# A fourth pair by seven products in nine feed-forward groups, two more weight slots, and the residual kept in DRAM meanwhile

## The chip, the cores and the metric

The kernel runs on one core of a Trainium2 chip. The metric is the device time of one execution in microseconds, as the median of several runs. Before the change it is 1207.95 us (three runs, 1207.74 to 1208.55).

## What is computed

One decoder layer on 256 tokens of width 2048, all in float32. A mixer (mLSTM and retention heads with a common input and output projection) comes first and is not touched by the change. The part that is:

```python
h = rmsnorm(x, g_ffn_pre[l])
ff = (jax.nn.silu(h @ w_gate[l]) * (h @ w_up[l])) @ w_down[l]
x = x + rmsnorm(ff, g_ffn_post[l])
```

`D_FF` is 5632, so `w_gate` and `w_up` are 2048 x 5632 and `w_down` is 5632 x 2048. `x` in the last line is the residual: the input plus the normed mixer output.

## The kernel before

**Products in parts.** Every operand of a matmul is split into a high part (rounded to the matmul's number format by a copy) and a low part (the value less its high part). A product A x B is then three matmuls: high x high, high x low, low x high. Activations are split once. Weights are split as they stream in: SyncE (SP) loads them from DRAM into `raw` (four chunks), ScalarE writes the high part to a slot of `w_hi` (ACT.Copy), VectorE subtracts and writes the low part to the same slot of `w_lo`, the TensorE multiplies and counts `sub_done`. There are `AHEAD = 4` slots of 128 x 1024; ScalarE may fill a slot again when `sub_done` says that the sub-block that used it is finished. Each engine takes its instructions in the order of its program.

**Groups.** The 5632 columns of gate and up are done in 11 groups of 512 (`FF_GROUPS`). Group 0 stands apart, in two plain rounds. Groups 1 to 10 go over the 2048 rows in eight *pairs* of 128-row tiles. The two weight matrices, the two tiles of a pair and the two halves of the tokens make a 2 x 2 by 2 x 2 block product for each pair. `Plan` (L59) says for each pair how it is done:
- "R": eight products, in two sub-blocks (up, then gate) of 12 matmuls of 128x512 each; 24 matmuls.
- "S": seven products of sums of blocks (a Strassen-Winograd scheme), in four pieces with 2, 1, 2 and 2 products; 6, 3, 6 and 6 matmuls, 21 together. The sums on the token side are made once per S pair, before group 1 (`seven_sums`, `seven_lo`). The sums on the weight side are made for each group anew, in `raw` itself.

Groups 1 to 9 use `FULL`, group 10 uses `FINAL`. `w_down` follows in two halves of 22 pairs (`DOWN`, `LAST_HALF`), six of them S in each; there the token sums are made along the way.

**An S pair, step by step.** The pair's raw chunk holds four blocks of 512 columns: b12, b22, b11, b21.
- ScalarE, `unit_hi` (L955): the high part of piece 0 (b22, b11), of piece 1 (b21), of piece 2 (after L622 and L1558), of piece 3 (after L624 and L626). The copy is on L976, for an R pair on L965.
- VectorE, `unit_lo` (L1541): the low part of piece 0 (L1550), then the sum L1558 (b12 + b11 after L622, written over b11), then the low parts of pieces 1, 2 and 3 (L1550). For an R pair: two low parts on L1547.
- GpSimd, `weight_sums` (L617): L622 (b22 - b12, as soon as the up half of the chunk has arrived), L624 (b22 - b11, after L1558), L626 (b21 - b11, after the low part of piece 1).
- TensorE, `seven_piece` (L2019): waits for the low part of each piece.

**The order within a group** is written out by hand in `ff_group`, once per engine. On VectorE (L1574), around the low parts of group i with number m: `partial_sums` of group i-1 before m = 1 (L1561), `up_sums` before m = 2, `gate_sums` before m = 3 (it waits until the TensorE has finished group i-1), `gated` before m = 4 (in group 1 `first_gated`, which waits for the whole round before), `turned_lo` after m = 5 (it follows eight transposes on the TensorE, L1986, and `turned_hi` on ScalarE). Before m = 4 there are always six R sub-blocks from pair 7 of the group before on.

**Loads.** SP issues them in order (`unit_rows`, L544): pair n + 4 is loaded into the chunk of pair n once VectorE has written the last low part of pair n. Up and gate halves are 512 KB each.

**The residual.** `resid` (L230, 16 KB per partition) holds x, from L1410 on x plus the mixer's result. The TensorE transposes it and ScalarE squares it while group 0 runs; nothing reads it after that until the last four adds for each token half (L1702), whose results SP stores to `out`.

Of the kernel before, what the change touches and what calls it, by code (L numbers as in the profile page):

```python
# [30 lines left out]
P = 128  # L31
SEQ = 256
# [23 lines left out]
SEVEN = (2, 4, 6)  # L56
# [13 lines left out]
FULL = Plan("RRSRSRSR")  # L70
FINAL = Plan("RRSRSRRR")
# [144 lines left out]
def hybrid_layer(nc, x, positions, g_mix_pre, w_in, conv_w, conv_b, b_igate, b_fgate, g_mlstm_head,  # L216
                 g_ret_head, w_out, g_mix_post, g_ffn_pre, w_gate, w_up, w_down, g_ffn_post,
                 inv_freq, out):
    with ExitStack() as ctx:
# [10 lines left out]
        resid = sb("resid", [P, TT, D])  # L230
# [77 lines left out]
        def s_upper(j):  # L308

            return s_hi[:, j] if j < 2 else s_third[:, 0]  # L310

        def s_lower(j):

            if j == 2:
                return s_third[:, 1, 0:2, :], s_third[:, 1, 2:4, :]
            return s_lo12(j), s_lo34[:, j]
# [88 lines left out]
        resid_ready = sem("resid_ready")  # L405
        h_ready = sem("h_ready")
# [72 lines left out]
        def _(sp):  # L479
# [163 lines left out]
        def _(act):  # L643
# [311 lines left out]
            def unit_hi(i, odd, plan, m):  # L955

                n, piece = plan.pieces[m]
                q, slot, arrived = chunk_of(i, n), ff_slot(i, odd, m), up_arrived(i, n)
                act.wait_ge(sub_done, ff_base(i) + (m - 3))
                if plan.units[n] == "R":  # L960
# [4 lines left out]
                    act.activation(w_hi[:, slot, :], raw[:, q, SUB * piece:SUB * (piece + 1)],  # L965
# [10 lines left out]
                act.activation(slot_blocks(w_hi, slot, piece), seven_blocks(piece, q),  # L976
# [1149 lines left out]
```

## Time and profile before

| | us |
|---|---|
| median of the runs | 1207.95 |
| the profiled execution | 1214.75 |
| its span, first to last instruction | 1213.0 |
| granted clock of the TensorE, mean | 0.997 |

The profile is of one execution. Times in it count from the first instruction. Engines: PE is the TensorE's matmul, PEld its weight load, DVE is VectorE, ACT is ScalarE, POOL is GpSimd, SPq is SyncE's queue of DMA issues. In a row of the timeline the first number is the start, the second the time taken (of several instructions, if it ends in x2 or x3), and the bracket at the end is the idle time of the engine before it, with what ended it. The rows in question stand below, in groups.

### The profile page before, as it was taken

How to read it: one execution, taken by the hardware profiler on the slowest of the kernel's cores; microseconds unless marked ns; L12 is line 12 of the kernel's file. 1: busy time of each engine (PE TensorE's matmuls, PEld its weight loads, DVE VectorE, ACT ScalarE, POOL GpSimd, SP SyncE). 2: the span in 40 equal slices, each digit the busy share in tenths (PEclk: the TensorE clock that was granted, in tenths of full speed). 3: DMA queues.
4: the chain of work that ended last, by engine and by line, in shares of the span. 5: the costliest groups of instructions: out<-in, count | busy, mean ns of one | idle time of the engine just before them, and what ended most of it. 6: DMA issues, size and time to landing. Idle time of an engine off the chain costs nothing.

```text
span 1213.0 us, 16357 instructions
## 1 busy us (share of the span) xinstructions
PE 1193.4 (98%) x5760; PEld 998.9 (82%) x5760; DVE 937.1 (77%) x1230; ACT 678.0 (56%) x896; POOL 214.3 (18%) x158
## 2 busy tenths in 40 slices
PE   8999999999899999999999999999999999999997
PEld 7888888888788888888888888888888878888885
DVE  6657777877677745868887888888788788879887
ACT  5654666474564744665556555555555555546553
POOL 1000100000000000004234333323433023313320
PEclk9999999999999999999999999999999999999999
DMA  8656867767676655545565566556556665564552
GB/s 314 210 148 159 213 180 150 180 142 198 163 163 184 216 200 187 180 158 203 187 208 169 202 207 207 193 187 211 172 206 208 212 215 206 197 210 158 206 199 98
DMA packets 122723, 230.67 MB, mean 190 GB/s; under 512 B 8104, under 2 KB 24752, under 8 KB 122032
## 3 DMA queue, kind: packets, MB, share of 16 engines
q1 hardware_dynamic: 122208, 226.85, 60.4%
q0 software_dynamic: 464, 3.15, 0.6%
q8 instruction: 30, 0.49, 0.2%
q14 instruction: 21, 0.17, 0.0%
HBM read 227.88 MB, written 2.11 MB: 190 GB/s over the span
## 4 chain that ended last, share of the span: by engine, by line
PE 89%; DMA 5%; DVE 3%; ACT 1%; issue 1%; POOL 0%; SPq 0%; DVEq 0%; ACTq 0%
PE bank L1709 88%; DMA raw<-in_w_in 4%; DVE w_lo L1067 1%; PE bank L1986 1%; DMA resid<-in_x 1%; ACT w_hi L656 1%; PE bank L1714 0%; PE bank L1903 0%; DVE h L1094 0%; DVE w_lo L1550 0%; DVE gT L1281 0%; DVE resid L1702 0%; ACT w_hi L976 0%; PE bank L1959 0%; DVE pre L1254 0%
## 5 line engine op out<-in xcount | busy, mean ns | idle before, releaser
L1709 PE MATMUL bank<-w_hi,h2T 128*128 128x512 f32 x1126 | 359.3, 390 | 0.0
L1067 DVE TENSOR_TENSOR w_lo<-raw,w_hi 128x1024 fp32r<-128x1024 f32 x172 | 209.7, 1224 | 131.4 <-ACT w_hi L656 130.6
L656 ACT ACTIVATE w_hi<-raw 128x1024 fp32r<-128x1024 f32 x172 | 180.6, 1058 | 181.6 <-PE bank L1709 154.8
L1550 DVE TENSOR_TENSOR w_lo<-raw,w_hi 128x1024 fp32r<-128x1024 f32 (+1 forms) x164 | 216.2, 1323 | 73.6 <-ACT w_hi L976 72.5
L1709 PE MATMUL bank<-hT,w_hi 128*128 128x512 f32 x768 | 271.3, 397 | 1.2 <-DVE w_lo L1067 1.2
L976 ACT ACTIVATE w_hi<-raw 128x1024 fp32r<-128x1024 f32 (+1 forms) x164 | 156.4, 954 | 168.0 <-PE bank L1709 139.9
L1709 PEld LDWEIGHTS bank<-w_hi,h2T 128*128 128x128 f32 x1126 | 211.4, 188 | 43.9
L1709 PE MATMUL bank<-hT,w_lo 128*128 128x256 f32 x768 | 214.6, 279 | 0.0
L1709 PE MATMUL bank<-w_lo,h2T 128*128 128x512 f32 x543 | 211.3, 389 | 0.0
L1547 DVE TENSOR_TENSOR w_lo<-raw,w_hi 128x1024 fp32r<-128x1024 f32 x166 | 198.0, 1224 | 15.8 <-ACT w_hi L965 14.3
L965 ACT ACTIVATE w_hi<-raw 128x1024 fp32r<-128x1024 f32 x166 | 169.9, 1055 | 67.3 <-PE bank L1709 65.0
L1709 PE MATMUL bank<-w_hi,ffT 128*128 128x512 f32 x584 | 184.3, 389 | 0.0
L1709 PEld LDWEIGHTS bank<-hT,w_hi 128*128 128x128 f32 x768 | 144.1, 188 | 33.6 <-DVE w_lo L1067 1.5
L1709 PEld LDWEIGHTS bank<-hT,w_lo 128*128 128x128 f32 x768 | 145.0, 189 | 0.0
L1709 PEld LDWEIGHTS bank<-w_hi,ffT 128*128 128x128 f32 x584 | 109.6, 188 | 23.0 <-DVE w_lo L1547 0.3
L624 POOL TENSOR_TENSOR raw<-raw 128x512 f32<-128x512 f32 x41 | 65.2, 1591 | 339.2 <-DVE raw L1558 339.2
L1709 PEld LDWEIGHTS bank<-w_lo,h2T 128*128 128x128 f32 x543 | 102.0, 188 | 21.0
L1709 PE MATMUL bank<-w_lo,ffT 128*128 128x512 f32 x292 | 113.6, 389 | 0.0
L622 POOL TENSOR_TENSOR raw<-raw 128x512 f32<-128x512 f32 x41 | 71.6, 1747 | 204.0 <-DMA raw<-in_w_up 189.5
L1709 PE MATMUL bank<-w_hi,hT 128*128 128x512 f32 x256 | 81.3, 393 | 0.9 <-DVE w_lo L1067 0.9
L1709 PE MATMUL bank<-w_hi,mixT 128*128 128x512 f32 x256 | 80.2, 391 | 0.0
L626 POOL TENSOR_TENSOR raw<-raw 128x512 f32<-128x512 f32 x41 | 66.5, 1623 | 6.3 <-DVE w_lo L1550 6.3
(232 smaller groups left out, 1264.4 us busy)
## 6 DMA issues: line engine op xcount, KB each, us to landing
raw<-in_w_in SPq DMA_DIRECT2D x63, 1024.0 KB, 10.6
raw<-in_w_down SPq DMA_DIRECT2D x88, 512.0 KB, 5.0
raw<-in_w_up SPq DMA_DIRECT2D x80, 512.0 KB, 4.0
raw<-in_w_gate SPq DMA_DIRECT2D x80, 512.0 KB, 4.8
raw<-in_w_out SPq DMA_DIRECT2D x16, 1024.0 KB, 5.1
raw<-in_w_gate SPq DMA_DIRECT2D x4, 1024.0 KB, 5.2
raw<-in_w_up SPq DMA_DIRECT2D x4, 1024.0 KB, 5.9
resid<-in_x SPq DMA_DIRECT2D x2, 1024.0 KB, 7.2
```

Source lines behind the costliest of these rows:

```text
L622: pool.tensor_tensor(b12, b22, b12, ALU.subtract).then_inc(t3_ready, 1)
L624: pool.tensor_tensor(b22, b22, b11, ALU.subtract).then_inc(t14_ready, 1)
L626: pool.tensor_tensor(b21, b21, b11, ALU.subtract).then_inc(t14_ready, 1)
L656: act.activation(part_of(w_hi, rnd, s), src, ACT.Copy).then_inc(hi_done, 1)
L965: act.activation(w_hi[:, slot, :], raw[:, q, SUB * piece:SUB * (piece + 1)], ACT.Copy).then_inc(hi_done, 1)
L976: act.activation(slot_blocks(w_hi, slot, piece), seven_blocks(piece, q), ACT.Copy).then_inc(hi_done, 1)
L1067: dve.tensor_tensor(part_of(w_lo, rnd, s), raw_sub(rnd, s)[1], part_of(w_hi, rnd, s).bitcast(F32), ALU.subtract).then_inc(lo_done, 1)
L1547: dve.tensor_tensor(w_lo[:, slot, :], raw[:, q, SUB * piece:SUB * (piece + 1)], w_hi[:, slot, :].bitcast(F32), ALU.subtract).then_inc(lo_d ...
L1550: dve.tensor_tensor(slot_blocks(w_lo, slot, piece), seven_blocks(piece, q), slot_blocks(w_hi, slot, piece).bitcast(F32), ALU.subtract)\
L1709: return pe.matmul(out_, lhsT, rhs, start=start, stop=stop, skip_group_check=True)
L1986: ins = pe.transpose(bank[:, b0 + j // 2, c:c + P], ff(t)[:, j * P:(j + 1) * P], ident)
```

## The change

- `SEVEN`, the S pairs of groups 1 to 9, goes from (2, 4, 6) to (2, 3, 5, 6), and `FULL` from RRSRSRSR to RRSSRSSR; a group has 24 sub-blocks and pieces in place of 22. `FINAL` (group 10) keeps two S pairs, now pairs 2 and 3.
- The slots of `w_hi` and `w_lo` go from four to six in the feed-forward part. The two new ones, `more_hi` and `more_lo`, lie over `resid`.
- SP copies `resid` to a DRAM scratch (two transfers of 1 MB) behind the loads of the first round and before those of group 1, and back when eight sub-blocks are left. ScalarE waits for the first (`spilled`) before it fills slot 4 the first time, VectorE for the second (`resid_back`) before the last adds. The last eight sub-blocks use four slots again.
- The token sums are made for four S pairs; the fourth's high and low parts (`s_fourth`) take the place of spare space.

The diff, cut to its core (what is left out passes the new slot lists to where `w_hi` and `w_lo` stood, drops an argument of `ff_slot`, and puts `len(SEVEN)` where 3 stood):

```diff
-SEVEN = (2, 4, 6)
+SEVEN = (2, 3, 5, 6)
+FF_SLOTS = 6
+END_SUBS = 8
...
-FULL = Plan("RRSRSRSR")
-FINAL = Plan("RRSRSRRR")
+FULL = Plan("RRSSRSSR")
+FINAL = Plan("RRSSRRRR")
...
+def at_end(i, m):
+
+    return isinstance(i, int) and i == FF_GROUPS + 1 and m >= DOWN.subs - END_SUBS
+
+
-def ff_slot(i, odd, m):
-
+def ff_slot(i, m):
+
+    if at_end(i, m):
+        return m % AHEAD
     if down_half(i) is not None:
-        return (ff_base(i) + m) % AHEAD
-    return (m + (0 if odd else FULL.subs)) % AHEAD
+        return (ff_base(i) + m - FF_FIRST) % FF_SLOTS
+    return m % FF_SLOTS
+
+
+def slot_depth(i, m, first=False):
+
+    return AHEAD if at_end(i, m) or (first and m < AHEAD) else FF_SLOTS
...
-        resid = sb("resid", [P, TT, D])
+        resid_home = ExitStack()
+        resid = sb("resid", [P, TT, D], stack=resid_home)
+        resid_home.close()
+        more_hi = sb("more_hi", [P, FF_SLOTS - AHEAD, SUB], F32R)
+        more_lo = sb("more_lo", [P, FF_SLOTS - AHEAD, SUB], F32R)
+        resid_rows = nc.dram_tensor("resid_rows", (SEQ, D), F32)
...
+            sp.wait_ge(resid_ready, TT * CHUNKS)
+            for t in range(TT):
+                sp.dma_start(resid_rows.ap()[t * P:(t + 1) * P, :], resid[:, t, :]).then_inc(spilled, 16)
             for n in range(4):
                 unit_rows(1, n, FF_FIRST - 8 + FREE[n])
...
+            sp.wait_ge(sub_done, N_SUBS - END_SUBS)
+            sp.wait_ge(spilled, 16 * TT)
+            for t in range(TT):
+                sp.dma_start(resid[:, t, :], resid_rows.ap()[t * P:(t + 1) * P, :]).then_inc(resid_back, 16)
...
-            def unit_hi(i, odd, plan, m):
+            def unit_hi(i, odd, plan, m, first=False):
 
                 n, piece = plan.pieces[m]
-                q, slot, arrived = chunk_of(i, n), ff_slot(i, odd, m), up_arrived(i, n)
-                act.wait_ge(sub_done, ff_base(i) + (m - 3))
+                q, slot, arrived = chunk_of(i, n), ff_slot(i, m), up_arrived(i, n)
+                if first and m >= AHEAD and m < FF_SLOTS:
+                    act.wait_ge(spilled, 16 * TT)
+                act.wait_ge(sub_done, ff_base(i) + (m + 1 - slot_depth(i, m, first)))
...
-                    if first and 1 <= m < 4:
+                    if first and 1 <= m <= len(SEVEN):
                         seven_lo(m - 1)
...
                 lo(R_FF + 1, s + AHEAD)
-                if s:
-                    seven_sums(s - 1)
+                seven_sums(s)
...
+                if t == 0:
+                    dve.wait_ge(resid_back, 16 * TT)
```

## Rows read from the trace of the kernel before

**Rows 1.** The page of the kernel before, busy time by engine.
```profile
PE 1193.4 (98%) x5760; PEld 998.9 (82%) x5760; DVE 937.1 (77%) x1230; ACT 678.0 (56%) x896; POOL 214.3 (18%) x158
```

**Rows 2.** The chain of waits, 560 to 980 us: start, us, what.
```profile
594.78 0.87 PE bank L1986 x8
595.66 41.74 PE bank L1709 x183
...
936.73 42.21 PE bank L1709 x186
```

**Rows 3.** Waits, whole span: us in total, times, longest us.
```profile
PEld bank L1709 <- DVE w_lo L1550: 5.0, 13, 1.0
```

**Rows 4.** Timeline of VectorE, 664 to 708: start, us, what, idle before.
```profile
664.70 3.49 DVE L1547 TENSOR_TENSOR w_lo<-raw,w_hi 128x1024 fp32r<-128x1024 f32 x3
...
677.87 1.22 DVE L1550 TENSOR_TENSOR w_lo<-raw,w_hi 128x1024 fp32r<-128x1024 f32 x1
...
686.30 2.35 DVE L1547 TENSOR_TENSOR w_lo<-raw,w_hi 128x1024 fp32r<-128x1024 f32 x2
688.58 1.21 DVE L1550 TENSOR_TENSOR w_lo<-raw,w_hi 128x1024 fp32r<-128x1024 f32 x1
...
696.84 2.35 DVE L1547 TENSOR_TENSOR w_lo<-raw,w_hi 128x1024 fp32r<-128x1024 f32 x2
699.11 1.21 DVE L1550 TENSOR_TENSOR w_lo<-raw,w_hi 128x1024 fp32r<-128x1024 f32 x1
700.35 0.69 DVE L1558 TENSOR_TENSOR raw<-raw 128x512 f32<-128x512 f32 x1
700.96 0.68 DVE L1550 TENSOR_TENSOR w_lo<-raw,w_hi 128x512 fp32r<-128x512 f32 x1
702.59 1.29 DVE L1550 TENSOR_TENSOR w_lo<-raw,w_hi 128x1024 fp32r<-128x1024 f32 x1 [0.95 <-ACT w_hi L976]
706.16 1.23 DVE L1550 TENSOR_TENSOR w_lo<-raw,w_hi 128x1024 fp32r<-128x1024 f32 x1 [2.28 <-ACT w_hi L976]
707.31 1.22 DVE L1547 TENSOR_TENSOR w_lo<-raw,w_hi 128x1024 fp32r<-128x1024 f32 x1
```

**Rows 5.** Timeline of GpSimd, 664 to 708: start, us, what, idle before.
```profile
701.12 1.68 POOL L624 TENSOR_TENSOR raw<-raw 128x512 f32<-128x512 f32 x1 [5.30 <-DVE raw L1558]
702.75 2.29 POOL L626 TENSOR_TENSOR raw<-raw 128x512 f32<-128x512 f32 x1
```

**Rows 6.** Line L626, 560 to 965: ns min/median/max.
```profile
L626 POOL TENSOR_TENSOR raw<-raw x28: 1277/1294/2297, 564.3 to 947.9; 128x512 f32<-128x512 f32 x28
```

**Rows 7.** Timeline of ScalarE, 698 to 708.
```profile
701.50 1.06 ACT L976 ACTIVATE w_hi<-raw 128x1024 fp32r<-128x1024 f32 x1 [2.10 <-PE bank L1709]
705.07 1.06 ACT L976 ACTIVATE w_hi<-raw 128x1024 fp32r<-128x1024 f32 x1 [2.51 <-POOL raw L626]
```

**Rows 8.** Groups by line, 560 to 1213: busy us, mean ns, idle before.
```profile
L976 ACT ACTIVATE w_hi<-raw 128x1024 fp32r<-128x1024 f32 x120 | 127.3, 1061 | 138.9 <-PE bank L1709 110.9 <-POOL raw L626 26.6
```

**Rows 9.** Loads from `in_w_up`, 500 to 540: ns, first and last start.
```profile
L485 SPq DMA_DIRECT2D raw<-in_w_up x2: 368/368/368, 507.8 to 512.2; - x2
```

**Rows 10.** The page, DMA issues: KB each, us to landing.
```profile
resid<-in_x SPq DMA_DIRECT2D x2, 1024.0 KB, 7.2
```

**Rows 11.** Timeline of ScalarE, 530 to 550.
```profile
546.86 1.06 ACT L976 ACTIVATE w_hi<-raw 128x1024 fp32r<-128x1024 f32 x1 [1.66 <-PE bank L1709]
```

**Rows 12.** Timeline of VectorE, 1165 to 1213.
```profile
1201.94 1.42 DVE L1702 SCALAR_TENSOR_TENSOR resid<-ff_out,stat,resid 128x512 f32<-128x512 f32 x2
```

**Rows 13.** Busy time by engine in one group: stretch, us, engines, PEclk, DMA, GB/s.
```profile
719.70:762.30 42.60, 42.60 (x193) 35.07 (x192) 35.90 (x38) 24.17 (x28) 14.55 (x9) 1.00 0.58 197
```

**Rows 14.** The same view around 312 us.
```profile
280.00:322.00 42.00, 38.75 (x219) 33.87 (x218) 27.36 (x36) 18.18 (x27) 0.00 (x0) 0.96 0.66 183
312.20:313.00 0.80, 0.78 (x3) 0.79 (x4) 0.80 (x1) 0.00 (x0) 0.00 (x0) 0.50 0.00 0
```

**Rows 15.** Timeline of the TensorE, 311.5 to 313.
```profile
312.22 1.01 PE L1709 MATMUL bank<-v_sb,probs 128*128 x3 [3.25 <-DVE probs L1309]
```

More of the change, by code:

```diff
@@ L308, in s_upper @@
         def s_upper(j):
-            return s_hi[:, j] if j < 2 else s_third[:, 0]
+            return s_hi[:, j] if j < 2 else (s_third, s_fourth)[j - 2][:, 0]
         def s_lower(j):
-            if j == 2:
-                return s_third[:, 1, 0:2, :], s_third[:, 1, 2:4, :]
+            if j >= 2:
+                lower = (s_third, s_fourth)[j - 2]
+                return lower[:, 1, 0:2, :], lower[:, 1, 2:4, :]
             return s_lo12(j), s_lo34[:, j]
@@ L321, in seven_blocks @@
             return (blocks[:, 1:3, :], blocks[:, 3:4, :], blocks[:, 0::2, :], blocks[:, 1::2, :])[piece]
+        hi_slots = [w_hi[:, s, :] for s in range(AHEAD)] + [more_hi[:, s, :] for s in range(FF_SLOTS - AHEAD)]
+        lo_slots = [w_lo[:, s, :] for s in range(AHEAD)] + [more_lo[:, s, :] for s in range(FF_SLOTS - AHEAD)]
+        early_hi_slots = [early[:, 0, s, :] for s in range(AHEAD)]
+        early_lo_slots = [early[:, 1, s, :] for s in range(AHEAD)]
         def slot_blocks(w, slot, piece):
-            return w[:, slot, :].rearrange("p (a c) -> p a c", c=512)[:, 0:1 if piece == 1 else 2, :]
+            return w[slot].rearrange("p (a c) -> p a c", c=512)[:, 0:1 if piece == 1 else 2, :]
         def s_lo12(j):
@@ L964, in unit_hi @@
                         act.wait_ge(raw_full[q], arrived + 16 * (R_FF + 2))
-                    act.activation(w_hi[:, slot, :], raw[:, q, SUB * piece:SUB * (piece + 1)],
+                    act.activation(hi_slots[slot], raw[:, q, SUB * piece:SUB * (piece + 1)],
                                    ACT.Copy).then_inc(hi_done, 1)
@@ L975, in unit_hi @@
                     act.wait_ge(t14_ready, 2 * sums_index(i, n) + 2)
-                act.activation(slot_blocks(w_hi, slot, piece), seven_blocks(piece, q),
+                act.activation(slot_blocks(hi_slots, slot, piece), seven_blocks(piece, q),
                                ACT.Copy).then_inc(hi_done, 1)
@@ L989, in ff_group @@
                         first_product(i - 1, FULL, c0)
-                    unit_hi(i, odd, plan, m)
+                    unit_hi(i, odd, plan, m, first)
                     if m == 0 and first:
-                        act.wait_ge(s_summed, 3)
-                        for j in range(3):
+                        act.wait_ge(s_summed, len(SEVEN))
+                        for j in range(len(SEVEN)):
                             act.activation(s_upper(j), s_sum[:, j], ACT.Copy).then_inc(s_rounded, 1)
@@ L1753, in wide_columns, with sub_tokens @@
                         after(s)
-            def sub_tokens(count, slot, act_T, pair, k0, last, tiles=range(TT), w_hi=w_hi, w_lo=w_lo):
+            def sub_tokens(count, slot, act_T, pair, k0, last, tiles=range(TT), w_hi=hi_slots, w_lo=lo_slots):
                 pe.wait_ge(lo_done, count)
@@ L1762, in sub_tokens @@
                         lo_x = act_T[:, k, SEQ + t * P:SEQ + (t + 1) * P]
-                        mm(bank[:, 2 * pair + t, :], hi_x, w_hi[:, slot, w], k == 0, False)
-                        mm(bank[:, 2 * pair + t, :], hi_x, w_lo[:, slot, w], False, False)
-                        ins = mm(bank[:, 2 * pair + t, :], lo_x, w_hi[:, slot, w], False, k == last)
+                        mm(bank[:, 2 * pair + t, :], hi_x, w_hi[slot][:, w], k == 0, False)
+                        mm(bank[:, 2 * pair + t, :], hi_x, w_lo[slot][:, w], False, False)
+                        ins = mm(bank[:, 2 * pair + t, :], lo_x, w_hi[slot][:, w], False, k == last)
                 if TT - 1 in tiles:
@@ L2014, in products @@
                 w = slice(512 * c, 512 * (c + 1))
-                mm(bank[:, b, :], act_hi, w_hi[:, slot, w], first, False)
-                mm(bank[:, b, :], act_hi, w_lo[:, slot, w], False, False)
-                return mm(bank[:, b, :], act_lo, w_hi[:, slot, w], False, False)
+                mm(bank[:, b, :], act_hi, hi_slots[slot][:, w], first, False)
+                mm(bank[:, b, :], act_hi, lo_slots[slot][:, w], False, False)
+                return mm(bank[:, b, :], act_lo, hi_slots[slot][:, w], False, False)
             def seven_piece(i, odd, plan, m, c0, s0):
                 n, piece = plan.pieces[m]
-                k, slot = 2 * n, ff_slot(i, odd, m)
+                k, slot = 2 * n, ff_slot(i, m)
                 half = down_half(i)
```

34 lines of the change are left out of this document (18 added, 16 removed).

## The prediction

> **What bounds the kernel now.** I read the totals first [rows 1]: the TensorE is busy for nearly the whole span, VectorE for three quarters. That points at the TensorE, and the chain of waits seems to agree: through the feed-forward part it is one unbroken run of matmuls [rows 2]. A group of eight pairs with three done by seven products takes 183 matmuls in 41.74 us (0.228 us each) and 0.87 us for eight transposes, 42.6 us together; group 10, with two such pairs, has 186 matmuls in 42.21 us, only 0.227 us each. So a little waiting hides in the longer pitch, and the list of waits says for what: the weight loads waited for VectorE's low part of a seven-product piece 13 times, 5.0 us in all [rows 3]. A TensorE that runs straight into its supplier, group after group, calls for a look at the supplier's own period.
>
> That is in VectorE's timeline of one group [rows 4]. I call a pair done by seven products an S unit, the other an R unit. From 664.70 to 707.31, one period of 42.61 us, VectorE does this, in its order:
> - 664.70 to 677.87, 13.17 us: six low parts of R units (L1547) and the sums of the group before (L1561 to L1508);
> - S unit to 686.30, 8.43 us (with `turned_lo`); R unit to 688.58, 2.28; S unit to 696.84, 8.26; R unit to 699.11, 2.27; S unit to 707.31, 8.20.
>
> There is no idle time outside the S units. The period of this in-order chain equals the TensorE's: the two engines bound the group together.
>
> What an S unit's 8.2 us consist of is seen in the third one [rows 4 to 7]. Low part of piece 0 at 699.11; sum L1558 (700.35 to 701.04); low part of piece 1 at 700.96. GpSimd's L624 starts at 701.12 and ends at 702.80, and its L626 at 702.75 takes 2.29 us, though the shortest takes 1.28 [rows 5, 6]. Low part of piece 2 runs 702.59 to 703.88; only then does L626 get on (703.88 + 1.2 = 705.04). ScalarE's high part of piece 3 starts at 705.07 [rows 7], VectorE's low part at 706.16. So VectorE and GpSimd take turns, each finishing its instruction before the other goes on, and piece 3 comes through GpSimd and ScalarE one after another. VectorE's five instructions last 5.1 us of the 8.2 [rows 4]; for the rest it stands still, in order behind piece 3.
>
> **The change, part by part.** Matmuls: an R unit has 24, an S unit 21. One more S unit in nine groups removes 27 matmuls x 0.228 = 6.2 us of TensorE work. Group 10 keeps two S units, only in other places.
>
> VectorE's chain: S for R adds 8.26 - 2.27 = 5.99 us a group. The new order RRSSRSSR gives 13.17 + 8.43 + 8.26 + 2.28 + 8.26 + 8.20 = 48.60 us [rows 4], against a TensorE need of 180 x 0.228 + 0.87 = 41.9. The chain wins: nine groups x 5.99 = +53.9 us, and none of the 6.2 us is seen, since the TensorE is then the one that waits. I take 8.26, the unit followed by another subtraction L622; the bounds of one S unit are worked out under the rivals (7.2) and by the slowest seen (8.43).
>
> Group 10: the TensorE enters it behind VectorE's last low part by six matmuls of a piece 3 and one R unit, less VectorE's own R unit: 30 x 0.228 - 2.28 = 4.6 us. VectorE needs (13.17 - 2.28) + 8.43 + 8.26 = 27.6 us to the end of the second, now adjacent, S unit, after which the TensorE has 6 + 4 x 24 = 102 matmuls, 23.2 us: 50.8 - 4.6 = 46.2 us instead of 42.21 + 0.87 = 43.1. That is +3.1 us.
>
> Two more slots (six for four): they let ScalarE's high parts start earlier. The view of waits has large figures for this: L976 waited 110.9 us for the TensorE to free a slot [rows 8]. In the third S unit the high part of piece 2 did so until 701.50 [rows 7]. But freed of it, it could start at 701.04, when L1558 is done, and be over at 702.1, while L624 holds VectorE off until 702.80 anyway. The slot wait is a shadow of another one. Slots lengthen the lead, they don't shorten the chain: worth at most one time two R sub-blocks, 2 x 12 x 0.228 = 5.5 us, in group 1. There VectorE waits for the whole round before (`first_gated`), so I take 0.
>
> Residual out: the spill stands on SP behind the loads of the first round, whose last issue is at 512.2 [rows 9]. A transfer of 1 MB took 7.2 us [rows 10]; that last load and both halves of the residual one after another end by 512.6 + 3 x 7.2 = 534 us. ScalarE needs the new slots first for its fifth high part of group 1, at 546.86 [rows 11]. Hidden, with 12 us to spare. Queued behind the spill on SP are the loads of group 1's first units; if they have no slack they come one or two transfers late, once: 0 taken, 14 at most. Residual back: queued once the last eight sub-blocks are left, 96 x 0.227 = 21.8 us before the TensorE ends, so about 1183; landed by 1198, needed at 1201.94 [rows 12]. Hidden too, with 4 us to spare. The wait in front of it on SP has only the output stores behind it. The fourth unit's token sums and their rounding come once, before and in group 1: seven VectorE operations, none wider than L1558 with its 0.69 us [rows 4], so under 4.8 us, in a stretch where VectorE waits for the TensorE in `first_gated`: 0 taken.
>
> **Sum.** 53.9 + 3.1 = +57 us. The profiled execution took 1214.75 us (span 1213.0); the median of the runs is 6.8 lower, and I carry the difference over: 1207.95 + 57 = 1265 us.
>
> Put strictly, as turns that never overlap, VectorE's operations on two SBUF tensors and GpSimd's must fit into a group one after another: 20 low parts x 1.14 us (686.30 to 688.58 is two), 8 operations of half the width x 0.61 (700.35 to 700.96), 12 on GpSimd x 1.28 [rows 4, 6] are 22.8 + 4.9 + 15.4 = 43.1 us, more than the TensorE's 41.9. The Trainium skill, "SBUF — State Buffer", section "Who interferes with whom", has this as a rule: with two SBUF inputs VectorE takes a read interface that GpSimd also needs, and the one that comes second is blocked. By that rule alone a group would be at least 43.1 us, a time between before and my forecast; the trace agrees with the turns and adds the dependences that make it 48.6.
>
> **The rivals.**
> A. *The forecast*, VectorE's chain at 8.26 us an S unit. For it: period equals period, waits of the TensorE only for that piece. With each of the 36 S units 0.4 us shorter or 0.3 longer it gives 1250 to 1276.
> B. *The TensorE stays the bound; faster.* VectorE's busy time in a group is 35.9 us [rows 13]; with an S unit's work in place of an R unit's about 39 of 41.9, so there is room if its idle time goes with the slots. The time would be 1207.95 - 6.2 = 1202, or 1197 if the 5.0 us of waits go as well. It decides where the four S units take no more than (41.9 - 13.17 - 2.28)/4 = 6.6 us each. Against it: slots don't touch L624, L626 and piece 3, which make the 8.2; and the turns alone need 43.1 of 41.9 us.
> C. *A shorter S unit.* If with a high part ready earlier L626 follows L624 at once, it ends at 702.80 + 1.28 = 704.1, low part of piece 2 at 705.2 beside the high part of piece 3, low part of piece 3 at 706.3: 7.2 us. The group is then 13.17 + 2.28 + 33.15 - 4 x 1.0 = 44.6, +2.0 for nine groups and about 1 in group 10: 1227. Against it: with the low part of piece 2 already waiting, VectorE went first.
> D. *The clock falls.* New gaps of the TensorE, up to about 2 us before a piece 3, 6.7 us a group. In the trace the granted clock fell to 0.50 (1.2 GHz) about 312 us, after a wait of 3.25 us [rows 14, 15]; a mean of 0.96 over 42 us makes that 3.4 us at the lower level. 1.7 us lost after each adjacent pair, 18 times: +31 on top of A, 1296. Against: my gaps are shorter, and the TensorE has slack to take it up. The Trainium skill, "TensorE: Matmul & The Clock Gate", section "A second HAM failure mode: psum-queue depth-cycling", reports a kernel whose short, repeated idling made the clock swing.
>
> **How the numbers follow.** A 0.68, B 0.08, C 0.15, D 0.07, and 0.02 for a result within 0.2% of before (about what a measurement of this kernel can tell from no change). The forecast is A's. The range leaves out B and most of D: 1220, a little under C, to 1286. Faster by over 0.2% 0.08, within it 0.02, slower 0.90.
>
> **What would show it.** Right: groups 2 to 9 about 48.6 us apart, VectorE's order without idle time outside S units, 8.2 to 8.4 us each; the TensorE waiting for VectorE's low part (seven-product form) some 60 us in all; fewer waits of ScalarE for slots with nothing gained. Wrong: groups 42 us apart with S units near 6.6 (B), 44 to 45 (C), clock records at 0.5 in the groups (D), a wait on the spill ahead of group 1's fifth high part, or of the last adds for the residual.

## The result, and the profile after

The kernel after takes 1268.77 us (median of 4 runs, 1268.35 to 1269.14) against 1207.85 for the kernel before: a ratio of 1.0503, interval 1.049 to 1.0516, +60.9 us. Its profiled execution took 1268.9 us with a span of 1267.1.

| | before | after | forecast |
|---|---|---|---|
| time, us | 1207.85 | 1268.77 | 1265 |
| one group of 2 to 9, us | 42.64 | 48.65 in five of eight, 49.4 in three | 48.60 |
| S unit on VectorE, us | 8.2 to 8.4 | 8.2 to 8.5 | 8.2 to 8.4 |

The code of the feed-forward part has moved by some 35 lines: `unit_lo` is L1583 (R) and L1586 (S), its sum L1594, `turned_lo` L1552, `gated` L1544, GpSimd's three sums L656, L658, L660, ScalarE's high parts L1001 (R) and L1012 (S), the matmul L1746.

The page of the kernel after, busy time by engine, answers to [rows 1]:

```profile
PE 1209.0 (95%) x5733; PEld 1001.9 (79%) x5733; DVE 970.8 (77%) x1264; ACT 679.1 (54%) x915; POOL 268.4 (21%) x185
```

There are 27 matmuls fewer and yet more busy time on the TensorE; VectorE has the same share as before. From this view alone nobody would call VectorE the bound. Its timeline over one group does it (start, time taken, what, idle time before), and answers to [rows 4]:

```profile
677.00 2.35 DVE L1583 TENSOR_TENSOR more_lo<-raw,more_hi 128x1024 fp32r<-128x1024 f32 x2
...
690.16 1.22 DVE L1586 TENSOR_TENSOR more_lo<-raw,more_hi 128x1024 fp32r<-128x1024 f32 x1
...
694.27 1.29 DVE L1552 TENSOR_TENSOR ffT<-bank,ffT 128x512 f32 x2 [1.45 <-ACT ffT L972]
695.48 4.36 DVE L1586 TENSOR_TENSOR w_lo<-raw,w_hi 128x1024 fp32r<-128x1024 f32 x3
...
706.92 2.35 DVE L1583 TENSOR_TENSOR w_lo<-raw,w_hi 128x1024 fp32r<-128x1024 f32 x2
709.19 1.22 DVE L1586 TENSOR_TENSOR w_lo<-raw,w_hi 128x1024 fp32r<-128x1024 f32 x1
710.53 0.69 DVE L1594 TENSOR_TENSOR raw<-raw 128x512 f32<-128x512 f32 x1
711.14 0.69 DVE L1586 TENSOR_TENSOR w_lo<-raw,w_hi 128x512 fp32r<-128x512 f32 x1
712.41 1.65 DVE L1586 TENSOR_TENSOR more_lo<-raw,more_hi 128x1024 fp32r<-128x1024 f32 x1 [0.59 <-ACT more_hi L1012]
716.33 1.23 DVE L1586 TENSOR_TENSOR more_lo<-raw,more_hi 128x1024 fp32r<-128x1024 f32 x1 [2.27 <-ACT more_hi L1012]
717.48 1.22 DVE L1586 TENSOR_TENSOR w_lo<-raw,w_hi 128x1024 fp32r<-128x1024 f32 x1
...
725.68 1.22 DVE L1583 TENSOR_TENSOR more_lo<-raw,more_hi 128x1024 fp32r<-128x1024 f32 x1
```

The period from 677.00 to 725.68 is 48.68 us: 13.16 for the R low parts and the group sums up to 690.16, then 16.76 for the first two S units with `turned_lo` between them, 2.27 for an R unit, 8.29 and 8.20 for the last two S units. All idle time is inside S units: the third one stands still 0.59 us before the low part of piece 2 and 2.27 us before that of piece 3, both times for ScalarE. GpSimd in the same stretch, which answers to [rows 5]:

```profile
711.30 1.68 POOL L658 TENSOR_TENSOR raw<-raw 128x512 f32<-128x512 f32 x1 [5.41 <-DVE raw L1594]
712.94 2.27 POOL L660 TENSOR_TENSOR raw<-raw 128x512 f32<-128x512 f32 x1
```

So L660 again takes 2.27 us: VectorE's low part of piece 2 starts first, at 712.41, in spite of the earlier high part, and L660 gets through after it. The TensorE now waits for this. The waits of its weight loads from 560 to 1060 us (total us, times, longest) answer to [rows 3]:

```profile
PEld bank L1746 <- DVE more_lo L1586: 32.9, 24, 2.3
PEld bank L1746 <- DVE w_lo L1586: 25.7, 17, 2.3
```

Over the whole span 5.0 us have become 59.9, of which 58.6 stand here. ScalarE's waits for a slot, [rows 8], are all but gone, and what stands in their place is what the prediction had called the real wait. The same list for ScalarE, 560 to 1040 us:

```profile
ACT more_hi L1012 <- POOL raw L660: 51.6, 18, 2.9
...
ACT more_hi L1012 <- DVE raw L1594: 43.1, 18, 2.9
...
ACT w_hi L1012 <- POOL raw L660: 25.6, 9, 2.9
```

The residual's round trip is hidden. From SP's queue and VectorE's timeline, the spill's issue, the issue of the way back and the first use of it:

```profile
505.77 1.40 SPq L586 DMA_DIRECT2D resid_rows<-resid  x2
...
1237.24 0.81 SPq L603 DMA_DIRECT2D resid<-resid_rows  x2
```

```profile
1256.04 1.42 DVE L1739 SCALAR_TENSOR_TENSOR resid<-ff_out,stat,resid 128x512 f32<-128x512 f32 x2
```

18.8 us lie between the last two, and VectorE's operation shows no idle time before it.

**Where the 60.9 us lie.** From the transposes of group 0 to the last `gate_sum_of` the profiled executions take 652.80 us before and 713.76 after, 60.96 more: group 1 +6.45; groups 2 to 9 together +50.49, which is 8 x 5.99 = 47.9 and 2.6 besides; group 10 +4.62; everything behind it -0.6. The 2.6, and the 1.5 in group 10 beyond its forecast, go with the clock, below.

**The clock.** Its mean fell from 0.997 to 0.985. The TensorE's timeline and then busy time by engine in short stretches (stretch, us, busy of PE, PEld, DVE, ACT and POOL, granted clock, DMA share, GB/s):

```profile
774.47 0.50 PE L1746 MATMUL bank<-w_hi,s_fourth 128*128 128x512 f32 x1 [1.84 <-DVE w_lo L1586]
```

```profile
776.00:779.00 3.00, 3.00 (x9) 2.32 (x8) 2.96 (x4) 2.53 (x5) 0.32 (x1) 0.50 0.95 338
779.00:782.00 3.00, 3.00 (x14) 2.45 (x14) 2.97 (x5) 0.91 (x1) 0.97 (x1) 0.99 0.92 323
```

The TensorE waited 1.84 us for the last piece 3 of its group, and from about 775.7 the clock was at 0.5 (1.2 GHz) for some 3.4 us, 9 matmuls in 3 us in place of 14. There are ten such falls between 560 and 1005 us. The waits ahead of them, 1.8 to 1.9 us, are shorter than the 3.25 us behind which the clock fell in the kernel before [rows 15]. Nine more waits of the same length in that stretch were followed by no fall. Most of the falls cost nothing, since the TensorE makes the loss good out of its next wait for VectorE. Three, at 629, 775.7 and 922, came behind the last such wait of a group: the eight transposes that follow were late, at 644.44, 791.22 and 937.98, and VectorE's `turned_lo` waited 3.0 us for them where it waits 1.4 otherwise. VectorE's timeline in one group of each kind:

```profile
793.25 1.29 DVE L1552 TENSOR_TENSOR ffT<-bank,ffT 128x512 f32 x2 [3.09 <-ACT ffT L972]
840.99 1.29 DVE L1552 TENSOR_TENSOR ffT<-bank,ffT 128x512 f32 x2 [1.38 <-ACT ffT L972]
```

The three groups with a late `turned_lo` are the ones that took 49.4 us: 0.8 each, 2.3 together. Another fall, at 1001 us, met group 10, where the TensorE waits no more.

### The profile page after: what moved, and what is told of

Same layout as the page of the kernel before. It is cut to its first block, busy times and chain, and to the rows that moved or that the text cites. A ratio compares the mean times of both kernels' runs of the same rounds, so it can differ in the third digit from the quotient of the medians.

```text
span 1267.1 us, 16472 instructions
## 1 busy us (share of the span) xinstructions
PE 1209.0 (95%) x5733; PEld 1001.9 (79%) x5733; DVE 970.8 (77%) x1264; ACT 679.1 (54%) x915; POOL 268.4 (21%) x185
## 4 chain that ended last, share of the span: by engine, by line
issue 53%; PE 29%; POOL 13%; DVE 2%; ACT 2%; DMA 1%; POOLq 0%; SPq 0%; DVEq 0%; ACTq 0%
PE bank L1746 29%; POOL raw L660 6%; POOL raw L656 4%; POOL raw L658 3%; DMA resid<-in_x 1%; POOL decay L644 0%; DVE w_lo L1586 0%; DVE w_lo L1103 0%; DVE more_lo L1586 0%; ACT w_hi L690 0%; ACT w_hi L1012 0%; DVE h L1130 0%; ACT more_hi L1012 0%; DVE resid L1739 0%; PE bank L1751 0%
## 5 line engine op out<-in xcount | busy, mean ns | idle before, releaser
L1103 DVE TENSOR_TENSOR w_lo<-raw,w_hi 128x1024 fp32r<-128x1024 f32 x172 | 209.7, 1225 | 123.0 <-ACT w_hi L690 122.3
L690 ACT ACTIVATE w_hi<-raw 128x1024 fp32r<-128x1024 f32 x172 | 180.9, 1058 | 175.0 <-PE bank L1746 157.5
L1746 PE MATMUL bank<-hT,w_hi 128*128 128x512 f32 x768 | 270.6, 396 | 0.0
L1746 PE MATMUL bank<-w_hi,h2T 128*128 128x512 f32 x778 | 259.4, 399 | 0.0
L1746 PE MATMUL bank<-hT,w_lo 128*128 128x256 f32 x768 | 214.6, 279 | 0.0
L1586 DVE TENSOR_TENSOR w_lo<-raw,w_hi 128x1024 fp32r<-128x1024 f32 x126 | 156.9, 1257 | 28.7 <-ACT w_hi L1012 27.6
L1746 PEld LDWEIGHTS bank<-w_hi,h2T 128*128 128x128 f32 x778 | 150.0, 193 | 31.8
L1746 PEld LDWEIGHTS bank<-hT,w_hi 128*128 128x128 f32 x768 | 143.9, 187 | 31.8 <-DVE w_lo L1103 0.2
L658 POOL TENSOR_TENSOR raw<-raw 128x512 f32<-128x512 f32 x50 | 85.9, 1718 | 342.7 <-DVE raw L1594 342.7
L1746 PE MATMUL bank<-w_lo,h2T 128*128 128x512 f32 x379 | 150.3, 396 | 0.0
L1012 ACT ACTIVATE w_hi<-raw 128x1024 fp32r<-128x1024 f32 x126 | 112.3, 931 | 62.3 <-POOL raw L660 41.5
L1746 PEld LDWEIGHTS bank<-hT,w_lo 128*128 128x128 f32 x768 | 145.0, 189 | 0.0
L1583 DVE TENSOR_TENSOR w_lo<-raw,w_hi 128x1024 fp32r<-128x1024 f32 x110 | 132.1, 1219 | 15.7 <-ACT w_hi L1001 15.3
L1586 DVE TENSOR_TENSOR more_lo<-raw,more_hi 128x1024 fp32r<-128x1024 f32 x74 | 97.2, 1314 | 55.6 <-ACT more_hi L1012 55.3
L1746 PE MATMUL bank<-w_hi,ffT 128*128 128x512 f32 x416 | 132.3, 389 | 0.0
L1012 ACT ACTIVATE more_hi<-raw 128x1024 fp32r<-128x1024 f32 x74 | 70.9, 974 | 107.2 <-POOL raw L660 60.8
L1001 ACT ACTIVATE w_hi<-raw 128x1024 fp32r<-128x1024 f32 x110 | 111.0, 1050 | 30.8 <-PE bank L1746 30.6
L656 POOL TENSOR_TENSOR raw<-raw 128x512 f32<-128x512 f32 x50 | 75.3, 1506 | 203.8 <-DMA raw<-in_w_up 189.8
L660 POOL TENSOR_TENSOR raw<-raw 128x512 f32<-128x512 f32 x50 | 97.2, 1945 | 1.0 <-DVE more_lo L1586 1.0
L1746 PE MATMUL bank<-more_hi,h2T 128*128 128x512 f32 x258 | 92.4, 417 | 0.0
L1746 PEld LDWEIGHTS bank<-w_hi,ffT 128*128 128x128 f32 x416 | 78.1, 188 | 16.2
L1746 PEld LDWEIGHTS bank<-w_lo,h2T 128*128 128x128 f32 x379 | 73.2, 193 | 15.5
```

Source lines behind the costliest of these rows:

```text
L656: pool.tensor_tensor(b12, b22, b12, ALU.subtract).then_inc(t3_ready, 1)
L658: pool.tensor_tensor(b22, b22, b11, ALU.subtract).then_inc(t14_ready, 1)
L660: pool.tensor_tensor(b21, b21, b11, ALU.subtract).then_inc(t14_ready, 1)
L690: act.activation(part_of(w_hi, rnd, s), src, ACT.Copy).then_inc(hi_done, 1)
L1001: act.activation(hi_slots[slot], raw[:, q, SUB * piece:SUB * (piece + 1)], ACT.Copy).then_inc(hi_done, 1)
L1012: act.activation(slot_blocks(hi_slots, slot, piece), seven_blocks(piece, q), ACT.Copy).then_inc(hi_done, 1)
```

## The experiments

What was in doubt: whether the two slots are worth anything, whether the round trip of the residual costs anything, and what makes an S unit 8.2 us long: dependences in VectorE's fixed order, or simply the sum of VectorE's and GpSimd's turns.

**The change with four slots.** `resid` keeps its place.

```diff
-FF_SLOTS = 6
+FF_SLOTS = 4
...
-            for t in range(TT):
-                sp.dma_start(resid_rows.ap()[t * P:(t + 1) * P, :], resid[:, t, :]).then_inc(spilled, 16)
```

> The changed kernel with four weight slots as before and the residual left at home: the fourth seven-product pair alone. Theory (VectorE's in-order chain sets the group): the slots are worth nothing once VectorE is the bound, groups 2 to 9 stay at 48.6 us, total 1267 to 1272 us. Rival (the slots are what keeps the cost down): groups above 49.5 us, total above 1277. Rival (the trip of the residual or the slots over it cost the time): back to 1202 to 1208.

Measured: 1280.29 us (1277.04 to 1282.96), ratio 1.0605, interval 1.0585 to 1.0625. The slots are worth 11.5 us to a kernel with four S units; I had taken 0, and of the two rivals the first came true. VectorE's timeline and, below it, ScalarE's show where (here L1572 and L998 are the S unit's low and high part):

```profile
668.00 2.27 DVE L1572 TENSOR_TENSOR w_lo<-raw,w_hi 128x1024 fp32r<-128x1024 f32 x1 [2.48 <-ACT w_hi L998]
```

```profile
666.91 1.06 ACT L998 ACTIVATE w_hi<-raw 128x1024 fp32r<-128x1024 f32 x1 [3.15 <-PE bank L1730]
```

Piece 2's high part waited until 666.91 for a slot, and VectorE stood 2.48 us where it stands 0.59 with six slots. A group took 48.65 us in two intervals and 50.1 to 51.0 in the other six. What tells the two kinds apart is the clock. Here it fell ten times as well, once just ahead of this wait (the first line; busy time by engine, granted clock, DMA share, GB/s). The second stretch lies in a group of 48.65 us, at the full clock, and the line of VectorE below it is the same piece 2 there:

```profile
661.50:664.90 3.40, 3.40 (x9) 2.62 (x9) 3.28 (x5) 1.42 (x2) 0.00 (x0) 0.50 0.83 270
692.10:715.00 22.90, 20.36 (x93) 16.30 (x92) 18.15 (x19) 11.75 (x15) 9.88 (x7) 1.00 0.44 144
```

```profile
715.84 1.36 DVE L1572 TENSOR_TENSOR w_lo<-raw,w_hi 128x1024 fp32r<-128x1024 f32 x1 [0.87 <-ACT w_hi L998]
```

So VectorE's chain keeps its 48.65 us with four slots too, as long as the clock holds. In all six longer groups `turned_lo` waited 3.0 us for transposes that came late, and where a fall also lay ahead of piece 2 of the third S unit, its slot came free late. A fall behind the last wait of a group costs the group 1.5 us with four slots and 0.8 with six. "The slot wait is a shadow" was right for a TensorE at its full clock; behind a fall it is the wait that comes last, and six slots take most of that up.

**The slots and the round trip alone**, with three S units as before.

```diff
-SEVEN = (2, 3, 5, 6)
+SEVEN = (2, 4, 6)
...
-FULL = Plan("RRSSRSSR")
-FINAL = Plan("RRSSRRRR")
+FULL = Plan("RRSRSRSR")
+FINAL = Plan("RRSRSRRR")
...
-    return AHEAD if at_end(i, m) or (first and m < AHEAD) else FF_SLOTS
+    return AHEAD if at_end(i, m) or (down_half(i) is None and m < AHEAD) else FF_SLOTS
```

> The kernel before (three seven-product pairs, old order) with the two more slots and the residual in DRAM; only the first four sub-blocks of each group still use a slot four sub-blocks later, because 22 does not divide by six. Theory: VectorE's chain needs 42.6 us a group with any number of slots, so at most the stalls of the second half go: 1204 to 1208 us, and a seven-product pair still takes VectorE 8.2 us. Rival (VectorE's idle time in such a pair comes from waiting for slots): it shrinks to 7.2 us or less, the TensorE's waits for low parts go, 1203. Rival (the residual's trip costs): 1210 or more.

Measured: 1206.70 us in 11 runs, ratio 0.9995, interval 0.9986 to 1.0004: no difference. ScalarE's waits for a slot in L1012 fell to 2.9 us, from 70.0 between 560 and 980 us in the kernel before, and in their place stand 51.4 for GpSimd and 48.0 for VectorE. The S unit did not get shorter, as VectorE's timeline shows:

```profile
695.66 1.63 DVE L1586 TENSOR_TENSOR w_lo<-raw,w_hi 128x1024 fp32r<-128x1024 f32 x1 [0.61 <-ACT w_hi L1012]
699.56 1.23 DVE L1586 TENSOR_TENSOR w_lo<-raw,w_hi 128x1024 fp32r<-128x1024 f32 x1 [2.27 <-ACT w_hi L1012]
```

The unit runs from 692.50 to 700.70, 8.20 us. That refutes rivals B and C, both of which wanted a shorter unit once slots are free, and it shows that the round trip of the residual is free.

**Two of GpSimd's three sums on VectorE**, in groups 1 to 10, in the kernel after.

```diff
                 pool.tensor_tensor(b12, b22, b12, ALU.subtract).then_inc(t3_ready, 1)
+                if down_half(i) is None:
+                    return
...
+                if piece == 1 and down_half(i) is None:
+                    b22, b11, b21 = (raw[:, q, 512 * c:512 * (c + 1)] for c in range(1, 4))
+                    dve.wait_ge(t2_ready, sums_index(i, n) + 1)
+                    dve.tensor_tensor(b22, b22, b11, ALU.subtract).then_inc(t14_ready, 1)
+                    dve.wait_ge(lo_done, ff_base(i) + (m + 1))
+                    dve.tensor_tensor(b21, b21, b11, ALU.subtract).then_inc(t14_ready, 1)
```

> The changed kernel with two of the three weight sums of each pair (b22 - b11, b21 - b11) moved from GpSimd to VectorE in groups 1 to 10, behind the low part of piece 1. All is still computed. Theory (what costs is the turn-taking with GpSimd and the way of piece 3 through it): a seven-product pair takes VectorE 1.2 + 3 x 0.61 + 0.65 + 2 x 1.14 = 6.0 us though VectorE does more work, group 13.17 + 1.2 + 2.28 + 24 = 40.7 us without any turn for the remaining sum on GpSimd and 44.5 with all four, TensorE need 41.9: total 1203 to 1232, most likely 1215. Rival (VectorE is short of capacity as such, its own work is too much): two more sums of 0.61 us in 38 pairs make it slower, 1268.8 + 46 = 1315.

Measured: 1214.87 us (1213.28 to 1217.16), ratio 1.006, interval 1.0046 to 1.0073. 53.9 of the 60.9 us are gone, by giving VectorE more work: 1015.1 us busy in place of 970.8. The last two S units of a group are 6.0 to 6.1 us long and have no idle time inside:

```profile
699.21 1.22 DVE L1588 TENSOR_TENSOR w_lo<-raw,w_hi 128x1024 fp32r<-128x1024 f32 x1
700.46 0.69 DVE L1596 TENSOR_TENSOR raw<-raw 128x512 f32<-128x512 f32 x1
701.07 0.68 DVE L1588 TENSOR_TENSOR w_lo<-raw,w_hi 128x512 fp32r<-128x512 f32 x1
701.67 0.68 DVE L1601 TENSOR_TENSOR raw<-raw 128x512 f32<-128x512 f32 x1
702.27 0.68 DVE L1603 TENSOR_TENSOR raw<-raw 128x512 f32<-128x512 f32 x1
702.88 2.44 DVE L1588 TENSOR_TENSOR w_lo<-raw,w_hi 128x1024 fp32r<-128x1024 f32 x2
705.23 2.35 DVE L1585 TENSOR_TENSOR more_lo<-raw,more_hi 128x1024 fp32r<-128x1024 f32 x2
```

That is the size of the cause: two sums that take VectorE 0.61 us each make the unit 2.2 us longer when GpSimd does them instead. A group takes 43.0 us in most cases and up to 43.9 in the worst; what is left over the TensorE's 41.9 is GpSimd's first sum (L656), which ran beside VectorE's low parts and took up to 2.14 us.

**All three sums on VectorE.** The same, and L656's sum in front of the low part of piece 1.

> As the run before it, with the third weight sum (b22 - b12) on VectorE too, so GpSimd has no part in groups 1 to 10. Theory: a pair takes 6.0 + 0.65 = 6.6 us, group 13.17 + 1.2 + 2.28 + 26.4 = 43.1 us, total 1207.9 + 9 x 0.5 + 1 = about 1213, with no VectorE instruction stretched beyond 1.25 us. Rival (capacity): 1268.8 + 38 x 3 x 0.61 = 1338.

Measured: 1212.53 us, ratio 1.0044, interval 1.003 to 1.0058; the group is 43.12 us in every group. VectorE is busy in all of it: 35.3 us of its own as after (20 full low parts x 1.14, 8 halves x 0.61, and 7.6 for the sums and `turned_lo`), 12 more halves x 0.61, and some 0.5 of waits for its own results. The bound is plain work now, 1.2 us over the TensorE.

**The first sum alone on VectorE**, the last two stay on GpSimd. This separates the two readings: it gives GpSimd four turns fewer in a group, but leaves every dependence of an S unit and lengthens VectorE's part.

```diff
+                if down_half(i) is not None:
+                    pool.wait_ge(raw_up[q], up_arrived(i, n))
+                    pool.tensor_tensor(b12, b22, b12, ALU.subtract).then_inc(t3_ready, 1)
...
+                    if down_half(i) is None:
+                        b12, b22 = raw[:, q, 0:512], raw[:, q, 512:1024]
+                        dve.tensor_tensor(b12, b22, b12, ALU.subtract).then_inc(t3_ready, 1)
```

> The kernel after, with the first of a pair's three remaining sums (b22-b12) done on VectorE in groups 1 to 10; the other two stay on GpSimd. Port-turn theory: the group is VectorE's own work plus about 1.2 us for each GpSimd sum that falls beside it. Per group four GpSimd sums go, three of which cost a turn (one per group runs beside VectorE's sums from PSUM): -3.6 us, and VectorE gains four operations of 0.61 us with some 0.1 us of waits each: +2.8 us. 48.68 becomes about 47.9, some 8 us over ten groups: 1257 to 1264. Chain theory (what bounds is the dependence ScalarE, VectorE, GpSimd, VectorE inside a pair, in which the first sum is beside the path): each pair gets 0.65 us longer and loses nothing, the group becomes 51.2, 1268.8 + 24 = 1290 to 1295.

Measured: 1286.42 us (1285.28 to 1288.04), ratio 1.0647, interval 1.0631 to 1.0663. A group takes 51.0 us. VectorE's timeline:

```profile
715.14 1.22 DVE L1587 TENSOR_TENSOR w_lo<-raw,w_hi 128x1024 fp32r<-128x1024 f32 x1
716.28 0.69 DVE L1595 TENSOR_TENSOR raw<-raw 128x512 f32<-128x512 f32 x1
717.00 0.69 DVE L1598 TENSOR_TENSOR raw<-raw 128x512 f32<-128x512 f32 x1
717.61 0.68 DVE L1587 TENSOR_TENSOR w_lo<-raw,w_hi 128x512 fp32r<-128x512 f32 x1
718.87 1.65 DVE L1587 TENSOR_TENSOR more_lo<-raw,more_hi 128x1024 fp32r<-128x1024 f32 x1 [0.58 <-ACT more_hi L1013]
722.79 1.23 DVE L1587 TENSOR_TENSOR more_lo<-raw,more_hi 128x1024 fp32r<-128x1024 f32 x1 [2.27 <-ACT more_hi L1013]
723.94 1.22 DVE L1587 TENSOR_TENSOR w_lo<-raw,w_hi 128x1024 fp32r<-128x1024 f32 x1
```

The unit is 8.80 us, 0.6 more, with the same 0.58 and 2.27 of idle time, and the fourth is 8.84. The chain of dependences sets the length of a unit, not the number of turns. That the group comes to 48.6 + 4 x 0.6 = 51.0 is in part luck: the clock fell in every group here, `turned_lo` waited 2.3 to 2.6 us for late transposes (2.50 at 700.59) where it waits 1.45 otherwise, and this stands where a turn of L656 (0.9 us) has gone. Even without that, at most 1.1 us, the group would be at about 50, against the 47.9 of the turns. The median of 1286.4 lies a little under the 1290 to 1295 of the chain theory; the reading of turns, 1257 to 1264, is refuted.

**Piece 3 one place later**, in the kernel before and in the kernel after: a low part of the next unit goes between pieces 2 and 3, on all engines, to fill the 2.27 us.

```diff
+                if kind == "S":
+                    at = self.base[n] + 3
+                    self.pieces[at:at + 2] = self.pieces[at + 1], self.pieces[at]
```

> The kernel before with piece 3 of each seven-product pair in groups 1 to 10 taken one place later on all engines, behind the first sub-block of the next pair. Theory: that sub-block's low part fills 1.14 us of VectorE's idle time in front of piece 3, the pair takes VectorE 7.1 us net, the group 39.2, and the TensorE bounds it: 1204 to 1206 us. Rival (the idle time is not VectorE waiting in order, but the ports or GpSimd being full): no change, 1207 to 1208, or slower.

> The changed kernel with piece 3 one place later. Theory: 1.14 us saved in each pair followed by an eight-product pair (two a group), 0.2 in the two followed by another seven-product pair, whose sum L1558 must wait for GpSimd: group 48.7 - 2.7 = 46.0, total about 1243. If GpSimd's and VectorE's turns alone bounded it, the group would be 44.4 and the total 1229; if nothing could be filled, 1269.

Measured: from before 1220.38 us, ratio 1.0103 (1.0087 to 1.0118); from after 1265.48, ratio 1.0477 (1.0461 to 1.0493). Both expectations missed, the first with the wrong sign; nearer came what each had beside it, that nothing changes or it gets slower, and that nothing can be filled (1269). One group of the kernel after, and one of its variant with piece 3 later (stretch, us, busy of PE, PEld, DVE, ACT and POOL, granted clock, DMA share, GB/s):

```profile
677.00:725.68 48.68, 44.26 (x188) 35.48 (x188) 38.14 (x41) 24.73 (x30) 19.72 (x12) 0.96 0.52 172
```

```profile
680.88:729.76 48.88, 44.69 (x189) 33.76 (x188) 44.09 (x41) 24.73 (x30) 23.68 (x12) 1.00 0.51 173
```

VectorE's idle time fell by 5.7 us and its busy time, with the same 41 instructions, rose by 6.0. The gap in which VectorE stood is the time in which GpSimd had its turns: an operation put there takes 2.2 to 2.3 us in place of 1.14, and GpSimd's sums take 2.2. So the chain and the turns lie close together in the kernel after: 12 sums x 1.2 us on top of VectorE's 35.3 make up to 49.7, and loosening one leaves the other. In the kernel before there is besides what the edit adds: the end of the last S unit is one sub-block later, `partial_sums` waits for it, and with four slots the next high part waits for a slot. The two waits are in the timeline (VectorE's, then ScalarE's); no run shows what each of them costs:

```profile
710.00 0.69 DVE L1573 TENSOR_TENSOR part<-part,bank 128x512 f32<-128x512 f32 x1 [2.14 <-ACT part L988]
```

```profile
691.27 1.06 ACT L971 ACTIVATE w_hi<-raw 128x1024 fp32r<-128x1024 f32 x1 [1.52 <-PE bank L1715]
```

**In search of a version that beats both.** In the kernel before, the two sums on VectorE as above:

> The kernel before with the weight sums b22 - b11 and b21 - b11 of groups 1 to 10 on VectorE. Theory: a seven-product pair takes VectorE about 6 us in place of 8.2, so its group needs 37 to 39 us and the TensorE alone bounds it at 183 x 0.2267 + 0.87 = 42.36 us instead of 42.63: nine groups x 0.27 = -2.4 us, total 1204 to 1206. Rival (VectorE's own work is what bounds): 29 pairs x 1.2 us more, 1230 or above.

Measured: 1206.01 us in 11 runs, ratio 0.9986, interval 0.9977 to 0.9995; a group takes 42.38 us in place of 42.64. The TensorE bounds it alone, and that is all its waits were worth.

In the kernel after, the last two sums on VectorE, and the first one on GpSimd only for pairs 2 and 3, where it runs beside VectorE's sums out of PSUM:

```diff
-                for n in SEVEN:
+                for n in SEVEN[:2]:
...
+                    if down_half(i) is None and n in SEVEN[2:]:
+                        b12, b22 = raw[:, q, 0:512], raw[:, q, 512:1024]
+                        dve.tensor_tensor(b12, b22, b12, ALU.subtract).then_inc(t3_ready, 1)
```

> The changed kernel with b22 - b11 and b21 - b11 on VectorE, and b22 - b12 on GpSimd for the first two seven-product pairs of a group, where it runs beside VectorE's sums from PSUM, on VectorE for the last two. Theory: against all sums on VectorE (43.12 us a group measured) 2 x 0.65 us less, so VectorE needs 41.8 us and the TensorE 41.9: the gain the change was after, 1207.5 - 9 x 0.7 = 1201 to 1204 us. If the turns with GpSimd cost as much as they spare: 1212.

Measured: 1208.15 us in 11 runs, ratio 1.0002, interval 0.9993 to 1.0011. The whole loss of the change is gone and nothing is won. Groups 2 to 9 take 42.6 to 43.1 us from transposes to transposes, 42.7 in the mean: the 41.9 is reached in none. VectorE was busy in 42.54 of the 43.00 us from 676 on, so that its own work fills the group. Placement does work where it is met; GpSimd's sum beside VectorE's operations with an input in PSUM takes 1.30 us, about the shortest seen [rows 6]:

```profile
706.53 1.30 POOL L656 TENSOR_TENSOR raw<-raw 128x512 f32<-128x512 f32 x1 [37.81 <-DMA raw<-in_w_up]
```

Last, four S pairs in the odd groups and three in the even ones, on top of the split sums, so that VectorE has room in every second group. In the first form pairs 2, 5 and 6 are S pairs in the even groups; pair 3, an R pair there, reads a token block in whose place the sums of its S form are kept (`s_lo12`), so that part of the result is another one, with the same work.

```diff
+EVEN = Plan("RRSRRSSR")
...
+                ff_group(Group(2 * j, j, False), False, EVEN)
+                ff_group(Group(2 * j + 1, j, True), True)
```

> A candidate to beat both kernels: odd groups 1 to 9 do four pairs by seven products, even groups 2 to 8 three; the last two sums of a pair on VectorE, the first on GpSimd for the pairs 2 and 3 and on VectorE for 5 and 6 (as in the run with split sums), six slots with the depth of four over a group's first four low parts. VectorE needs about 42.1 us in an odd group (as measured with split sums where nothing was late) and about 4 less in an even one, TensorE 41.7 and 42.4, so TensorE should bound all: 42.1 a group in the mean against 42.7, 1202 to 1205. If late transposes or contended sums cost as much as with split sums alone: 1206 to 1208.

> The alternating plan with another choice of pairs in the even groups: 2, 3 and 6 by seven products (pairs 2, 3, 5 and 6 in the odd ones), so that pair 3, whose token block of h2T holds sums, is never computed plainly. TensorE bounds it: the run with the other choice had 42.99 us in an interval with an even plan and 42.01 in one with an odd plan, with VectorE busy 39.2 and 41.6 of them. Expected the same 42.5 in the mean against 42.64 of the kernel before, so 1206 to 1207.5; 1202 or less if the odd and even intervals can come down to the 41.7 us that TensorE was busy in an odd one; 1210 or more if two adjacent pairs in an even group make low parts late.

Measured, 11 runs each: 1206.70 us, ratio 0.999 (0.9981 to 0.9999), and 1207.36, ratio 0.9996 (0.9987 to 1.0005). The first lies 0.1% under the kernel before, but part of its result is another one; the second, which computes the whole layer, can't be told from before. In the second form, one interval with four S pairs and one with three:

```profile
703.49:746.48 42.99, 42.72 (x192) 34.81 (x191) 41.74 (x51) 25.52 (x30) 1.29 (x1) 1.00 0.53 170
746.48:788.74 42.26, 42.26 (x191) 34.74 (x190) 37.81 (x46) 23.19 (x28) 3.88 (x3) 1.00 0.66 225
```

42.6 in the mean. With 42.38 us for a group with three S pairs and two sums on VectorE, as measured, and a need of 41.9 with four, a mixed plan could at best reach 42.1; the groups with four took 43.0 in place of 41.9, and that takes all of it.

## Why the prediction was right

**The mechanism and its main term.** VectorE's in-order chain took over as forecast: 48.65 us measured against 48.60 summed from [rows 4], no idle time outside the S units, and the TensorE waiting 59.9 us for "some 60". 5.99 us for S in place of R holds to two hundredths where nothing else interferes (48.65 - 42.64 = 6.01). The time was 3.8 us over the forecast, 1268.8 against 1265.

**Group 10, +3.1 forecast, +4.6 measured**, and 2.6 us more in groups 2 to 9. Both come from the clock, for which the sum had no term. Rival D named the fall, but priced it as a loss of the TensorE's (+31 us). Measured, the falls were there, ten of them, and most ran in slack. The price is in what VectorE waits for, the transposes: 0.8 us where a fall came between the last wait of a group and these, three times, and some 1.5 us in group 10. About 4 us in all, not 31. The kernel with four slots bears this out: no fall met its group 10, and that took 46.1 us from transposes to transposes (995.88 to 1041.96), where the sum had 46.2; in the kernel after it took 47.7.

**"Slots worth 0"** was right of the chain and left the clock out. In the kernel before the slots alone change nothing, and with four slots the groups of the changed kernel that no fall touched took 48.65 us, as with six. But behind a fall four slots come free late, and with ten falls the kernel with four takes 11.5 us more. The forecast came out because the change brings the slots along; that it came out with no term for the clock at all is in part luck.

**Turns or dependences.** The prediction held both and counted dependences, and the run with the first sum on VectorE bears that out (51.0 us, as the dependences say). The strict bound of 43.1 us was too low: it left out VectorE's other work (L1544, and the sums and `turned_lo` that read PSUM, 7.6 us), which the in-order engine must do too. VectorE's own 35.3 and GpSimd's 12 x 1.2 make 49.7 if nothing overlaps, 48.5 if one of the twelve runs beside sums out of PSUM, against a measured 48.65 in the kernel after and 48.9 with piece 3 later. The Trainium skill, "SBUF — State Buffer", section "Who interferes with whom", says that a VectorE instruction with two SBUF inputs contends with GpSimd's reads and that one with at most one SBUF input does not; the runs agree in both halves, 2.27 us for a sum beside low parts and 1.30 beside sums out of PSUM. With both engines' whole work put in, the sum of turns comes within 1 us of what was measured.

**Rivals.** B and C are refuted by the run with slots alone: 8.20 us an S unit with slot waits gone. B's point of decision, 6.6 us a unit with `turned_lo` in the first, was near the mark: with two sums on VectorE the units come to 6.9 us in the mean (27.6 us for four) and the group to 43.0, 1.1 over the TensorE's need. What kept them above the limit are the turns of L656, which the last two units, at 6.0 to 6.1 us, don't have.

**Round trip, token sums, spill.** Nothing of these is seen, as forecast. The way back was issued 18.8 us ahead of its use.

**The 6.8 us carried over.** The profiled execution of before was 6.8 us over the median, and I carried that. By the traces it lay ahead of the feed-forward part: group 0's transposes came 6.9 us later than in the profile after (552.11 and 545.24). ScalarE's waits for loads of `in_w_in` were 26.6 us there, 17.2 in the profile after, and the clock fell once, after a wait of 3.25 us [rows 15], at a price of some 1.7 us (3.4 us at half the clock). Carrying it was right.

**Not tried:** a kernel without the clock's falls and otherwise the same, so that the 4 us, and the part of the clock in the 11.5 us of the slots, are read from the timelines, group by group, and not from a run. The kernel with piece 3 later kept its mean clock at 0.998, but it differs in more than that.

## What to carry to other kernels

An optimisation of TensorE's work is worth only what its supplier can follow: lay the supplier's in-order timeline of one period beside the bound engine's before removing work from the latter. A helper engine that takes a small operation off a busy one may cost it more than it saves, if both need the same read path and the result is waited for in order: here a unit took 2.2 us less once VectorE did two sums of 0.61 us itself. And a wait that is a shadow today can be the real one once the change lets the clock fall, so price a buffer in the state after the change.

## What was unexpected of the hardware

The granted clock fell to 1.2 GHz for about 3.4 us behind waits of under 2 us (1.84 us at 774.47). The Trainium skill, "TensorE: Matmul & The Clock Gate", section "A second HAM failure mode: psum-queue depth-cycling", reports a kernel in which short idling between matmuls, often repeated, makes the clock swing; this trace agrees with ten falls, though nine other waits of 1.8 to 1.9 us had none behind them. The kernel with piece 3 later waited as well, in more and shorter pieces (the longest 1.4 us), and its clock did not fall between 560 and 1040 us.

VectorE's idle time was GpSimd's working time: filling 5.7 us of it a group raised VectorE's busy time by 6.0 us and moved the period by 0.2.
